# The recurrence of a two-model kernel: second running sum right behind the first, the next step's readers between the two groups of level 1, last-column copies in eight entries

## The chip, the cores and the metric

The kernel runs on one core of a Trainium2 chip. Its engines are TensorE (PE for the matmuls, PEld for the loads of their stationary operand), VectorE (DVE), ScalarE (ACT), GpSimd (POOL) and the queue of SyncE (SP) that issues most transfers. They run side by side and wait for one another by semaphores. The metric is the device time of one execution in microseconds (us), lower is better.

## The reference

The reference is two small models, one after the other. What the change touches is one stage of the first: the RWKV recurrence, run once forward and once backward over 256 context tokens and then 512 image tokens, with a 64x64 state for each of 16 heads.

```python
def wkv_scan(r, decay, k, v, a_vec, b_vec, s0, reverse):
    def step(s, inp):
        r_t, w_t, k_t, v_t, a_t, b_t = inp
        sa = jnp.einsum('bhvk,bhk->bhv', s, a_t)
        s = s * w_t[:, :, None, :] + sa[..., None] * b_t[:, :, None, :] + v_t[..., None] * k_t[:, :, None, :]
        return s, jnp.einsum('bhvk,bhk->bhv', s, r_t)
    ...
            for d in range(N_DIRS):
                reverse = d == 1
                dec_c, k_c, a_c = dirs_c[d]
                yc_d, s_ctx = wkv_scan(r_c, dec_c, k_c, vh_c, -kk_c, kk_c * a_c, s0, reverse)
                dec_x, k_x, a_x = dirs_x[d]
                yx_d, _ = wkv_scan(r_x, dec_x, k_x, vh_x, -kk_x, kk_x * a_x, s_ctx, reverse)
```

## The kernel before

The tokens are cut into chunks of 64: four of context, then eight of the image. A step n (0 to 11) works on a pair of chunks, one of each direction, numbered u = 2n (forward) and u = 2n + 1 (backward). Within a chunk the recurrence is a triangular solve, done by doubling in levels 1 to 5, each level in two groups g of four head pairs. One level of one group is: TensorE's factor (L2427), ScalarE's copies of it out of PSUM (L2251, L2253, L2254), TensorE's update (L2444), VectorE's add of that (L2340) and VectorE's transpose (L2344), which the factor of the next level reads. Below, update(l, g) is that add on VectorE.

While step n goes through its levels, two other things are woven in, by an order that is written out by hand for each engine (`wkv_tensor`, `wkv_scalar`, `wkv_vector`, `wkv_pool`):

- the rest of step n - 1 (`before`): its right sides, its solution, its outputs (L2535 on TensorE; copied by ScalarE at L2273 for the first half of the image, added by VectorE at L2356 for the second) and its new states (L2552; added by VectorE at L2364);
- the preparation of step n + 1 (`after`), for each of its two chunks: `chunk_scan` (a running sum of log decays on VectorE, L2155), `chunk_rise` and `chunk_fall` (the exponentials of it and of its negative on ScalarE, L2108 and L2113), `chunk_readers` on VectorE (a product L2167, in image chunks a second one L2169, and a copy L2171 of the last column into PT), `chunk_writers` (two products, L2182), the score matmuls (L2218), and on GpSimd the masks of the scores (`chunk_mask`, L2094 and L2096, and `chunk_strict`, L2101).

Once a step GpSimd multiplies the states with the last columns (`decay`, L2229). It runs behind the masks in GpSimd's queue and reads PT. PT has four entries, so `chunk_readers` waits for a decay before it writes:

```python
                for step in (last, f"zn{u - 4}"):
                    if later(dve, step):
                        dve.wait_ge(*at(step))
```

`last` is the last output (image) or right side (context) of step n - 1, which reads the same buffer that the readers write. Transfers of a chunk's streams into LD are issued by SP as soon as the writers of that buffer are done; `chunk_scan` waits for them (`ld{u}`).

Of the kernel before, what the change touches and what calls it, by code (L numbers as in the profile page):

```python
# [25 lines left out]
P = 128  # L26
# [10 lines left out]
CH = 64  # L37
# [131 lines left out]
def build(nc, a, out, table):  # L169
# [3 lines left out]
    with ctx:  # L173
# [1831 lines left out]
        def take_scr(*dims):  # L2005
            nonlocal off
            t = S(off, *dims)
            off += int(np.prod(dims))
            return t
# [3 lines left out]
        EM = [EPX[0][:, :, 0:CH], EPX[1][:, :, 1:CH + 1]]  # L2013
        BK = [take_scr(KT, 2, CH) for _ in range(2)]
        MD = take_scr(2, 128)
        PT = take_scr(4, 8)
        assert off <= 12288 + 10 * TA
        off = 12288 + 10 * TA
        ZZ = take_scr(2, 8, CH)
# [137 lines left out]
        def chunk_readers(dve, u, d, c, img, first):  # L2157
            ld = LD[:, d]
            if later(dve, f"rise{u}"):
                dve.wait_ge(*at(f"rise{u}"))  # L2160
            if u >= 4:
                last = f"Y{u - 4}.1" if u - 4 >= 2 * NCHC else f"Q{u - 4}.1"
                for step in (last, f"zn{u - 4}"):
                    if later(dve, step):
                        dve.wait_ge(*at(step))
            r = AR[(u // 2) % 2][d]
            did(V, dve.scalar_tensor_tensor(r[:, :, 0, :], v3(ld[:, 2, :]), -1.0, EM[d], ALU.mult, ALU.mult).then_inc(vector_done, 1))  # L2167
            if img:
                did(V, dve.tensor_tensor(r[:, :, 1, :], v3(ld[:, 5, :]), EP[d], ALU.mult).then_inc(vector_done, 1))  # L2169
            e = CH - 1 if d == 0 else 0  # L2170
            did(V, dve.tensor_copy(PT[:, u % 4, :], EP[d][:, :, e]).then_inc(vector_done, 1))  # L2171

        def chunk_writers(dve, u, d, c, img, first):
            ld = LD[:, d]
# [48 lines left out]
        def wkv_pool(pool):  # L2223
            steps = list(units())

            def decay(u):
                if later(pool, f"free.Z{u}.1"):
                    pool.wait_ge(*at(f"free.Z{u}.1"))
                did(G_, pool.tensor_tensor(ZZ[:, :, :, :], ZZ[:, :, :, :], PT[:, u % 4:u % 4 + 2, :].unsqueeze(3).to_broadcast([P, 2, 8, CH]),  # L2229
                                           ALU.mult).then_inc(pool_done, 1), f"zn{u}")  # L2230
                marks[f"zn{u + 1}"] = marks[f"zn{u}"]
            for n, pair in list(enumerate(steps))[1:]:
                if n >= 2:
                    decay(2 * (n - 2))
                for un in pair:
                    chunk_mask(pool, un, 0)
                    chunk_mask(pool, un, 1)
                for l in range(2, LEVELS):
                    for un in pair:
                        chunk_mask(pool, un, l)  # L2240
                for un in pair:
                    chunk_strict(pool, *un)
            decay(2 * (NCH - 2))

        def wkv_scalar(act):
            def factor(pair, l, g):
                for u, d, c, img, first in pair:
                    t = pairs(tile(act, f"G{u}.{l}.{g}"))
                    out = GT[d][:, 4 * g:4 * g + 4, :]
                    if d == 0:  # L2250
                        did(A_, act.activation(out, t, ACT.Copy).then_inc(scalar_done, 1), f"free.G{u}.{l}.{g}")  # L2251
                    else:
                        did(A_, act.activation(out[rows(0)], t[rows(1)], ACT.Copy).then_inc(scalar_done, 1))  # L2253
                        did(A_, act.activation(out[rows(1)], t[rows(0)], ACT.Copy).then_inc(scalar_done, 1), f"free.G{u}.{l}.{g}")  # L2254

            def right_side(pair, g):
                for u, d, c, img, first in pair:
                    t = tile(act, f"Q{u}.{g}")
                    did(A_, act.activation(QB[d][:, 4 * g:4 * g + 4, :], pairs(t), ACT.Copy).then_inc(scalar_done, 1), f"free.Q{u}.{g}")

            def solution(pair, g):
                for u, d, c, img, first in pair:
                    sv = SV[u // 2 % 2][d]
                    t = pairs(tile(act, f"S{u}.{g}"))
                    for q in range(2):
                        did(A_, act.activation(sv[q][rows(1 - q), 4 * g:4 * g + 4, :], t[rows(1 - q)], ACT.Copy).then_inc(scalar_done, 1))
                    marks[f"free.S{u}.{g}"] = (A_, count[A_])

            def first_outputs(pair, g):
                for u, d, c, img, first in pair:  # L2270
                    if img and first:
                        t = pairs(tile(act, f"Y{u}.{g}"))
                        did(A_, act.activation(YA[:, 4 * g:4 * g + 4, c * CH:c * CH + CH], t, ACT.Copy).then_inc(scalar_done, 1), f"free.Y{u}.{g}")  # L2273

            def keys(u, d, c, img, first):
                for q in range(2):
                    t = tile(act, f"T{u}.{q}")
                    did(A_, act.activation(odd(BKT[d], q), t.rearrange("p (h c) -> p h c", c=CH), ACT.Copy).then_inc(scalar_done, 1), f"free.T{u}.{q}")
            steps = list(units())
            for n in range(NCH + 1):  # L2280
                now = steps[n] if n < NCH else []
                before = steps[n - 1] if n else []
                after = steps[n + 1] if n + 1 < NCH else []
                right_side(before, 0)
                right_side(before, 1)
                solution(before, 0)
                factor(now, 1, 0)
                solution(before, 1)
                first_outputs(before, 0)
                factor(now, 1, 1)  # L2290
                first_outputs(before, 1)
                if after:
                    chunk_rise(act, *after[0])
                    chunk_fall(act, *after[0])
                factor(now, 2, 0)
                if after:
                    chunk_rise(act, *after[1])
                factor(now, 2, 1)
                factor(now, 3, 0)
                if now:  # L2300
                    keys(*now[0])
                factor(now, 3, 1)
                if now:
                    keys(*now[1])
                if after:
                    chunk_fall(act, *after[1])
                factor(now, 4, 0)
                if after:
                    chunk_evict(act, *after[0], (0,))
                factor(now, 4, 1)  # L2310
                if after:
                    chunk_evict(act, *after[0], (1,))
                factor(now, 5, 0)
                if after:
                    chunk_evict(act, *after[1])
                factor(now, 5, 1)

        def wkv_vector(dve):
# [48 lines left out]
            for n in range(NCH + 1):  # L2367
                now = steps[n] if n < NCH else []
                before = steps[n - 1] if n else []
                after = steps[n + 1] if n + 1 < NCH else []  # L2370
                if n and now:
                    chunk_begin(dve, *now[1])
                    first_turn(dve, now)
                update(before, 5, 1)
                if after:
                    chunk_scan(dve, *after[0])
                outputs(before, 0)
                update(now, 1, 0)
                outputs(before, 1)
                update(now, 1, 1)  # L2380
                if after:
                    chunk_scan(dve, *after[1])
                states(before if now else [], 0)
                update(now, 2, 0)
                states(before if now else [], 1)
                update(now, 2, 1)
                if after:
                    chunk_readers(dve, *after[0])
                update(now, 3, 0)
                if after:  # L2390
                    chunk_writers(dve, *after[0])
                update(now, 3, 1)
                if after:
                    chunk_readers(dve, *after[1])
                update(now, 4, 0)
                if after:
                    chunk_writers(dve, *after[1])
                    lower(*after[0], (0,))
                update(now, 4, 1)
                if after:  # L2400
                    lower(*after[0], (1,))
                if after:
                    lower(*after[1], (0,))
                update(now, 5, 0)
                if after:
                    lower(*after[1], (1,))
                    chunk_begin(dve, *after[0])
# [1599 lines left out]
```

## Time and profile before

| | |
|---|---|
| time, 3 runs | median 3513.45 us (3512.17 to 3514.84) |
| the profiled execution | 3511.41 us, span 3509.6 us |
| recurrence in the trace | from about 1205 us to about 1630 us |
| one step | 30.6 us (step 0) to 40.5 us (step 9), by the starts of the first running sum |
| busy over the span | PE 94%, DVE 41%, ACT 33%, POOL 10% |

The share of busy time says little here: PE counts as busy in other stages too, and inside the recurrence four engines take turns. What counts is which result the others are waiting for at a given place of a step. In the trace a step is found by its running sums: step 5, which is shown most below, starts with the one at 1372.34 us.

### The profile page before, as it was taken

To read this page: it belongs to the slowest core of one execution; us is meant where nothing else is said; L and a number is where in the kernel's file an instruction comes from. 1 tells how busy PE (TensorE), PEld (TensorE's weight loads), DVE (VectorE), ACT (ScalarE), POOL (GpSimd) and SP (SyncE) were. 2 spreads that over 40 slices of the span, in tenths; PEclk is the share of its full clock that TensorE was granted. 3 is DMA by queue.
4 is the path that set the end of the run, shared out by engine and by line. 5 is a ranking of instruction groups with operands and counts; after the bars stand their busy time and mean duration, and the time that the engine had idled before them with its cause. 6 is when DMAs were issued, how large, how long until landed. Compare 5 with 4: busy or idle time off the path is not lost.

```text
span 3509.6 us, 63853 instructions
## 1 busy us (share of the span) xinstructions
PE 3294.7 (94%) x28640; PEld 2166.4 (62%) x28640; DVE 1427.5 (41%) x2203; ACT 1163.9 (33%) x2220; POOL 362.9 (10%) x294
## 2 busy tenths in 40 slices
PE   8999999999899998888888888899999999999998
PEld 6665444435458588886342332457788876778886
DVE  3341000024651378785420001467743445764343
ACT  3330111113451477764200001345331324533231
POOL 0010000000200275653000000010000001000000
PEclk9989999999999999999999999999999999999999
DMA  9268999995543444335379999521423212142320
GB/s 373 97 244 332 393 372 385 370 351 197 184 164 117 123 90 98 84 82 184 130 296 419 421 408 421 213 67 55 144 96 93 87 31 68 55 144 96 96 84 24
DMA packets 340209, 674.78 MB, mean 192 GB/s; under 512 B 156616, under 2 KB 248904, under 8 KB 284640
## 3 DMA queue, kind: packets, MB, share of 16 engines
q1 hardware_dynamic: 328048, 633.14, 49.8%
q0 software_dynamic: 5264, 18.68, 1.5%
q10 hardware_dynamic: 6624, 18.88, 1.4%
q8 instruction: 225, 3.69, 0.4%
q14 instruction: 48, 0.39, 0.0%
HBM read 636.04 MB, written 34.60 MB: 191 GB/s over the span
## 4 chain that ended last, share of the span: by engine, by line
PE 78%; DVE 8%; DMA 8%; ACT 3%; POOL 2%; issue 1%; SPq 0%; ACTq 0%; DVEq 0%; POOLq 0%
PE ps L1180 15%; PE ps L1191 5%; DMA ring<-in_moe_wu 4%; PE ps L3578 3%; PE ps L685 3%; PE ps L3577 3%; PE ps L3576 3%; PE ps L686 3%; PE ps L687 3%; PE ps L3595 3%; PE ps L3593 3%; PE ps L3594 3%; PE ps L1727 2%; PE ps L1702 2%; DMA ring<-in_moe_wg 2%; PE ps L769 2%
## 5 line engine op out<-in xcount | busy, mean ns | idle before, releaser
L1180 PE MATMUL ps<-ring,H 128*64 128x512 f32 x2016 | 479.8, 601 | 40.3 <-DMA ring<-in_moe_wu 31.7
L1312 DVE TENSOR_TENSOR scr<-ps,scr 128x512 f32<-128x512 f32 x32 | 22.1, 692 | 884.6 <-PE ps L1180 884.6
L1180 PEld LDWEIGHTS ps<-ring,H 128*64 128x64 f32 x2016 | 150.4, 137 | 324.4 <-issue 237.9
L1180 PE MATMUL ps<-ring,scr 128*64 128x512 f32 x1016 | 244.3, 599 | 29.2 <-DMA ring<-in_moe_wd 25.1
L3558 DVE TENSOR_TENSOR ring_rounded<-ring,scr_rounded 128x2048 fp32r<-128x2048 f32 x64 | 146.7, 2292 | 215.0 <-ACT scr_rounded L3551 214.6
L3578 PE MATMUL ps<-scr_rounded 128*128 128x512 f32 x512 | 203.4, 397 | 0.0
L3593 PE MATMUL ps<-scr_rounded,ring_rounded 128*128 128x512 f32 x512 | 201.6, 394 | 1.7 <-DVE ring_rounded L3558 1.7
L3595 PE MATMUL ps<-scr_rounded 128*128 128x512 f32 x512 | 202.9, 396 | 0.0
L3577 PE MATMUL ps<-H_rounded,scr_rounded 128*128 128x512 f32 x512 | 202.2, 395 | 0.0
L3551 ACT ACTIVATE scr_rounded<-ring 128x2048 fp32r<-128x2048 f32 x64 | 122.1, 1907 | 241.1 <-PE ps L3595 241.1
L3576 PE MATMUL ps<-scr_rounded,ring_rounded 128*128 128x512 f32 x512 | 200.5, 392 | 0.0
L1180 PEld LDWEIGHTS ps<-ring,scr 128*64 128x64 f32 x1016 | 74.5, 137 | 176.3 <-issue 125.9
L1259 ACT ACTIVATE scr<-ps 128x512 f32<-128x512 f32 x32 | 19.1, 597 | 383.2 <-PE ps L1219 383.2
L686 PE MATMUL ps<-H_rounded,ring_rounded 128*128 128x512 f32 (+1 forms) x384 | 143.3, 373 | 0.0
L1269 ACT ACTIVATE scr<-ps 64x512 f32<-64x512 f32 x64 | 37.9, 592 | 287.6 <-PE ps L1180 286.8
L1191 PE MATMUL ps<-ring,H 128*32 128x256 f32 x2048 | 120.3, 381 | 0.0
L687 PE MATMUL ps<-ring_rounded 128*128 128x512 f32 (+1 forms) x320 | 118.5, 370 | 0.0
L3615 ACT ACTIVATE scr<-ps 128x512 f32<-128x512 f32 x64 | 38.3, 598 | 226.8 <-PE ps L3578 226.8
L2427 PE MATMUL ps<-scr,ring 64*64 64x64 f32 x3840 | 93.4, 226 | 20.8 <-issue 9.2
L3577 PEld LDWEIGHTS ps<-H_rounded,scr_rounded 128*128 128x128 f32 x512 | 96.1, 188 | 25.6 <-issue 0.5
L3576 PEld LDWEIGHTS ps<-scr_rounded,ring_rounded 128*128 128x128 f32 x512 | 96.1, 188 | 24.4 <-issue 0.5
L3593 PEld LDWEIGHTS ps<-scr_rounded,ring_rounded 128*128 128x128 f32 x512 | 96.1, 188 | 24.1 <-issue 2.1
(548 smaller groups left out, 6694.6 us busy)
## 6 DMA issues: line engine op xcount, KB each, us to landing
ring<-in_moe_wu SPq DMA_DIRECT2D x128, 1024.0 KB, 9.6
ring<-in_moe_wd SPq DMA_DIRECT2D x127, 1024.0 KB, 10.2
ring<-in_moe_wg SPq DMA_DIRECT2D x124, 1024.0 KB, 9.7
ring<-in_mlp_w SPq DMA_DIRECT2D x64, 1024.0 KB, 5.4
ring<-in_ada_w SPq DMA_DIRECT2D x48, 1024.0 KB, 10.6
ring<-in_w_in SPq DMA_DIRECT2D x14, 1024.0 KB, 5.3
ring<-in_w_out SPq DMA_DIRECT2D x8, 1024.0 KB, 5.3
st_lw<-scr POOLq DMA_DIRECT2D x16, 384.0 KB, 3.9
```

The source lines that it names most:

```text
L685: pe.matmul(out, w[1], x[0], start=start, stop=False)
L686: pe.matmul(rest or out, w[0], x[1], start=False, stop=False)
L687: return pe.matmul(out, w[0], x[0], start=False, stop=stop)
L1180: ins = pe.matmul(bx[64 * n:64 * n + 64, :], stat_x(k), w[:, k % 4, :], start=k == 0, stop=k == KT - 1)
L1191: ins = pe.matmul(bc[32 * n:32 * n + 32, 0:256], stat_c(k), w[:, k % 4, o:o + 256], start=k == 0, stop=k == KT - 1)
L3551: did(A_, act.activation(WHI[j % 2], ring[:, place[name][0], :], ACT.Copy).then_inc(scalar_done, 1), f"wh.{name}")
L3558: did(V, dve.tensor_tensor(ring_r[:, at_slot, :], ring[:, at_slot, :], WHI[j % 2].bitcast(F32), ALU.subtract).then_inc(vector_done, 1), f" ...
L3576: pe.matmul(b, low[:, k, o], hh, start=k == 0, stop=False)
L3577: pe.matmul(b, high[:, k, o], hl, start=False, stop=False)
L3578: ins = pe.matmul(b, high[:, k, o], hh, start=False, stop=k == KT - 1)
L3593: pe.matmul(banks[m], low[:, k, o], hh, start=f == 0, stop=False)
L3595: ins = pe.matmul(banks[m], high[:, k, o], hh, start=False, stop=f == 15)
```

## The change

Four edits, all in the recurrence. On VectorE the running sum of the second chunk (`chunk_scan(dve, *after[1])`) moves from behind update(1, 1) to directly behind that of the first chunk. The readers of the first chunk move from behind update(2, 1) to between update(1, 0) and the outputs and update(1, 1). On ScalarE the rising exponential of the first chunk moves ahead of the second group of the outputs. PT gets eight entries instead of four, and `chunk_readers` waits for the decay eight chunks back, not four.

```diff
-        PT = take_scr(4, 8)
+        PT = take_scr(8, 8)
...
-                for step in (last, f"zn{u - 4}"):
+                for step in (last, f"zn{u - 8}")[0:1 + (u >= 8)]:
...
-            did(V, dve.tensor_copy(PT[:, u % 4, :], EP[d][:, :, e]).then_inc(vector_done, 1))
+            did(V, dve.tensor_copy(PT[:, u % 8, :], EP[d][:, :, e]).then_inc(vector_done, 1))
...
                 factor(now, 1, 1)
+                if after:
+                    chunk_rise(act, *after[0])
                 first_outputs(before, 1)
                 if after:
-                    chunk_rise(act, *after[0])
                     chunk_fall(act, *after[0])
...
                 if after:
                     chunk_scan(dve, *after[0])
+                    chunk_scan(dve, *after[1])
                 outputs(before, 0)
                 update(now, 1, 0)
+                if after:
+                    chunk_readers(dve, *after[0])
                 outputs(before, 1)
                 update(now, 1, 1)
-                if after:
-                    chunk_scan(dve, *after[1])
                 states(before if now else [], 0)
                 update(now, 2, 0)
                 states(before if now else [], 1)
                 update(now, 2, 1)
-                if after:
-                    chunk_readers(dve, *after[0])
                 update(now, 3, 0)
```

VectorE before, from the last update of step 4 to update(3, 0) of step 5 (in the order of the program the running sum is printed as SCALAR_TENSOR_TENSOR at L2155):

```order
L2340 TENSOR_TENSOR scr<-ps,scr 128x512
L2155 SCALAR_TENSOR_TENSOR scr<-scr,H 128x512
L2340 TENSOR_TENSOR scr<-ps,ring 128x512
L2344 STREAM_TRANSPOSE scr<-scr 128x512
L2340 TENSOR_TENSOR scr<-ps,ring 128x512
L2344 STREAM_TRANSPOSE scr<-scr 128x512
L2155 SCALAR_TENSOR_TENSOR scr<-scr,H 128x512
L2364 TENSOR_TENSOR scr<-ps,scr 128x2x256
```

VectorE with the change, the same place (every line behind the edit has one number more, L2341 is the former L2340):

```order
L2341 TENSOR_TENSOR scr<-ps,scr 128x512
L2155 SCALAR_TENSOR_TENSOR scr<-scr,H 128x512 x2
L2341 TENSOR_TENSOR scr<-ps,ring 128x512
L2345 STREAM_TRANSPOSE scr<-scr 128x512
L2167 SCALAR_TENSOR_TENSOR scr<-H,scr 128x8x64
L2169 TENSOR_TENSOR scr<-H,scr 128x8x64
L2171 COPY scr<-scr 128x8
L2341 TENSOR_TENSOR scr<-ps,ring 128x512
L2345 STREAM_TRANSPOSE scr<-scr 128x512
L2365 TENSOR_TENSOR scr<-ps,scr 128x2x256
```

Both running sums now stand ahead of update(1, 0), and the three instructions of the readers stand ahead of update(1, 1).

ScalarE, steps 5 to 8, the one piece that differs (L2254 ends the copies of level 1, L2273 is the outputs' second group):

```order
 L2253 ACTIVATE ring<-ps 64x256
 L2254 ACTIVATE ring<-ps 64x256
+L2108 ACTIVATE scr<-scr 128x8x64
 L2273 ACTIVATE scr<-ps 128x4x64 x2
-L2108 ACTIVATE scr<-scr 128x8x64
 L2113 ACTIVATE scr<-scr 128x512
```

The rising exponential now stands ahead of the two copies of the outputs, so it no longer waits for them. TensorE's and GpSimd's orders are the same.

## Rows read from the trace of the kernel before

**Rows 1.** Waits, 1200 to 1630 us: total us, times, longest us.
```profile
DVE scr L2340 <- PE ps L2444: 61.2, 44, 4.7
...
PEld ps L2427 <- issue: 21.0, 23, 4.4
...
ACT scr L2113 <- DVE scr L2182: 7.0, 9, 1.7
...
DVE X L2167 <- POOL scr L2229: 4.0, 4, 1.6
```

**Rows 2.** Timeline of step 5, all engines: start, length, instruction, [idle before <- releaser].
```profile
1377.65 0.69 DVE L2340 TENSOR_TENSOR scr<-ps,ring 128x512 f32<-128x512 f32 x1 [3.92 <-PE ps L2444]
...
1378.12 0.38 ACT L2254 ACTIVATE ring<-ps 64x256 f32<-64x256 f32 x1
...
1379.28 0.85 ACT L2273 ACTIVATE scr<-ps 128x256 f32<-128x256 f32 x2 [0.79 <-PE ps L2535]
...
1380.83 0.69 DVE L2340 TENSOR_TENSOR scr<-ps,ring 128x512 f32<-128x512 f32 x1 [1.74 <-PE ps L2444]
...
1381.55 0.71 DVE L2344 STREAM_TRANSPOSE scr<-scr 128x512 f32<-128x512 f32 x1
...
1382.19 1.18 DVE L2155 TENSOR_TENSOR_SCAN scr<-scr,H 128x512 f32<-128x512 f32 x1
...
1383.13 0.27 PE L2427 MATMUL ps<-scr,ring 64*64 64x64 f32 x2
...
1386.08 0.69 DVE L2340 TENSOR_TENSOR scr<-ps,scr 128x512 f32<-128x512 f32 x1 [0.21 <-PE ps L2444]
...
1387.96 0.69 DVE L2167 SCALAR_TENSOR_TENSOR X<-H,scr 128x512 f32<-128x512 f32 x1 [0.44 <-POOL scr L2229]
...
1389.17 0.16 DVE L2171 COPY scr<-scr 128x8 f32<-128x8 f32 x1
1389.24 0.68 DVE L2340 TENSOR_TENSOR scr<-ps,scr 128x512 f32<-128x512 f32 x1
...
1391.88 0.63 ACT L2113 ACTIVATE scr<-scr 128x512 f32<-128x512 f32 x1 [0.60 <-DVE scr L2182]
```

**Rows 3.** Timeline of POOL in the same step.
```profile
1366.77 12.95 POOL L2094 TENSOR_TENSOR ring<-scr 128x512 f32<-128x512 f32 x9
1379.67 2.54 POOL L2101 TENSOR_TENSOR scr<-scr 128x512 f32<-128x512 f32 x2
```

**Rows 4.** Timeline of DVE in step 0.
```profile
1208.49 0.69 DVE L2340 TENSOR_TENSOR scr<-ps,ring 128x512 f32<-128x512 f32 x1 [0.34 <-PE ps L2444]
...
1212.47 1.23 DVE L2155 TENSOR_TENSOR_SCAN scr<-scr,H 128x512 f32<-128x512 f32 x1 [1.22 <-DMA H<-st_kk]
...
1216.39 0.69 DVE L2340 TENSOR_TENSOR scr<-ps,scr 128x512 f32<-128x512 f32 x1 [1.36 <-PE ps L2444]
```

**Rows 5.** Timeline of the steps 3 and 9.
```profile
1307.07 0.63 ACT L2108 ACTIVATE scr<-scr 128x512 f32<-128x512 f32 x1
...
1307.82 0.69 DVE L2340 TENSOR_TENSOR scr<-ps,ring 128x512 f32<-128x512 f32 x1 [0.90 <-PE ps L2444]
...
1527.30 0.89 DVE L2356 TENSOR_TENSOR scr<-ps,scr 128x256 f32<-128x256 f32 x2
```

**Rows 6.** Timeline of two later stages, DVE and POOL.
```profile
1648.58 1.27 POOL L2651 TENSOR_TENSOR scr<-scr 128x512 f32<-128x512 f32 x1 [2.93 <-DMA scr<-st_kd]
1648.66 1.74 DVE L2679 SCALAR_TENSOR_TENSOR scr<-scr,cst 128x512 f32<-128x512 f32 x1
...
1653.65 0.75 DVE L2679 SCALAR_TENSOR_TENSOR scr<-scr,cst 128x512 f32<-128x512 f32 x1
...
1749.12 9.27 POOL L1620 TENSOR_TENSOR scr_rounded<-scr,scr_rounded 128x1024 fp32r<-128x1024 f32 x4 [92.70 <-ACT scr_rounded L1462]
...
1756.78 1.89 DVE L1527 TENSOR_SCALAR scr<-scr 16x512 f32<-16x512 f32 x1
```

**Rows 7.** Groups by line and form, DVE: xcount, then busy us, mean ns, idle before.
```profile
L1163 DVE TENSOR_SCALAR scr<-scr,small 16x512 f32<-16x512 f32 x2 | 0.9, 474 | 0.1
```

More of the change, by code:

```diff
@@ L2228, in decay @@
                     pool.wait_ge(*at(f"free.Z{u}.1"))
-                did(G_, pool.tensor_tensor(ZZ[:, :, :, :], ZZ[:, :, :, :], PT[:, u % 4:u % 4 + 2, :].unsqueeze(3).to_broadcast([P, 2, 8, CH]),
+                did(G_, pool.tensor_tensor(ZZ[:, :, :, :], ZZ[:, :, :, :], PT[:, u % 8:u % 8 + 2, :].unsqueeze(3).to_broadcast([P, 2, 8, CH]),
                                            ALU.mult).then_inc(pool_done, 1), f"zn{u}")
```

## The prediction

> **What bounds the kernel now.** I read the waits of the stretch first, then one step's timeline with all engines, then GpSimd alone. The waits [rows 1] show VectorE waiting 61.2 us in 44 places for update matmuls: in most of a step VectorE has time, and only where it is late is a shorter order worth something. Step 5 [rows 2] shows where. VectorE is idle 3.92 us ahead of update(1, 0) and 1.74 us ahead of update(1, 1). Behind update(1, 1) it is busy nearly without a gap: transpose, running sum (1.18 us at 1382.19), states, update(2, 0), and at update(2, 1) a wait of only 0.21 us for TensorE. So the running sum there stood beside TensorE's own chain and cost almost nothing. Then come the readers, 0.44 us late for GpSimd's decay, and update(3, 0) starts at 1389.24 with no wait for TensorE: from here VectorE is what the others wait for. ScalarE stands 0.60 us ahead of L2113 for VectorE's writers. In all steps this last wait is 7.0 us in 9 places [rows 1].
>
> **What the change frees.** It takes the second running sum, the first readers and the wait for the decay out of the late part of a step. What that is worth is not their length but what the next bound leaves. In step 5 update(3, 0) and the writers behind it come earlier, ScalarE can start L2113 as soon as its copies of the keys are done, and that is those 0.60 us; from there the copies of level 4 and TensorE's update of level 4 follow it. So the gain over all steps is 7.0 us, plus what comes earlier because ScalarE no longer waits for the second running sum ahead of its copies of level 2. Working steps 1 and 3 through by their rows in the same way as step 5, I get 0.2 and 0.5 us for that; rounded up for the others, 0.9. Gain: 7.9 us, at least 7.0. The sum in its new place lies in the 3.92 us ahead of update(1, 0) and costs nothing in the steps from 1 on; with that cover gone it would cost its 1.2 us. The eight entries of PT and the copy's new address cost nothing by themselves.
>
> **What it costs in step 0.** There the second running sum starts at 1212.47, when its streams have landed, 1.22 us after VectorE was ready, while both updates of level 1 had been done from 1208.49 on [rows 4]. With the sum ahead of them, update(1, 0) cannot start before 1212.47 + 1.14 = 1213.6, which is 5.1 us later. Everything of levels 1 and 2 is queued behind that instruction. Update(2, 1) had waited 1.36 us behind the same late sum by way of ScalarE; that wait is gone, so 5.1 - 1.4 = 3.7 us remain. Bounds: 3.7 to 5.1.
>
> **What the readers cost in their new place.** Update(1, 1) started at 1380.83 and its transpose ended at 1381.55 + 0.71 = 1382.26; TensorE's factor of the next level came at 1383.13 [rows 2]. So update(1, 1) can be late by 0.87 us before TensorE feels it.
>
> In step 5 the readers must wait for the outputs that read their buffer; ScalarE's row at 1379.28 shows when these are there. The rising exponential, moved ahead, runs from 1378.12 + 0.38 on and is done by then. Alone the three instructions take 1389.24 - 1387.96 = 1.28 us and end at 1380.56, inside the gap. In steps 3 and 4 there is no such cover: the exponential comes at 1307.07 + 0.63 = 1307.70 and update(1, 1) had been at 1307.82 [rows 5], so it slips by 1.2 us. In steps 9 and 10 the outputs of VectorE (L2356, from 1527.30) stand behind the readers, which costs 0.6 us, still under 0.87.
>
> But GpSimd is at work there. Before, the readers ran when its masks were done; now they run at 1379.3 to 1382, and the masks and strict masks fill 1366.77 to 1382.2 [rows 3], some 1.2 us more once the second sum runs beside them. Two rows show what an op with two inputs in SBUF does beside a GpSimd product [rows 6]: the same L2679 takes 0.75 us alone and 1.74 us when GpSimd's 1.27 us product began at 1648.58, 0.08 us ahead of it. It stood still for 0.99 us. So I charge 0.5 us for the first product of a chunk's readers (it meets a GpSimd op half way on the mean) and 1.0 us for a second one, since GpSimd's next mask is queued and starts when the first product ends.
>
> For the copy of the last column the rows don't decide. It took 0.16 us [rows 2], always with GpSimd idle or behind it. Of ops with one input, the transpose kept its 0.71 us while GpSimd ran [rows 2, 3], but L1527 took 1.89 us beside GpSimd's products [rows 6], where a tensor-scalar op of the same 16x512 took 0.474 [rows 7]. A copy from SBUF to SBUF is nearer to L1527 than to the transpose, so I charge it one wait of 1.0 us; bounds 0 and 1.4.
>
> The Trainium skill has a rule for this place, and it speaks against the change: "SBUF — State Buffer", section "SBUF: two separate sides", says that VectorE and GpSimd share a port pair under an exclusive lock, which a VectorE op takes when it has two SBUF inputs or is in a two-port mode, and that the loser stands still for a whole instruction. "VectorE: DVE Perf Modes", section "What auto-detection actually checks", puts a one-source op with source and destination in SBUF into such a mode, a copy too. By these the copy is held as well; L2679 and L1527 agree. By the idle rows alone the readers would cost no more than their 1.28 us, and the sum would be the faster rival below.
>
> Lateness of update(1, 1), less the 0.87 us, and less what steps 3 and 4 pay even unheld (0.35 us, already in the gain):
> - steps 1 and 2 (one product and a copy): 0.6 + 0.5 + 1.0 = 2.1, so 1.25 each, 2.5
> - steps 3 and 4: 1.2 + 1.5 + 1.0 = 3.7, so 2.5 each, 5.0
> - steps 5 to 8: 1379.28 + 1.28 + 2.5 = 1383.06, which is 2.23 late, so 1.36 each, 5.4
> - step 9: 0.6 + 2.5 = 3.1, so 2.2; step 10, where GpSimd's work ends before the copy, 1.2: 3.4
> Together 16.3 us, of which 9.0 are the copies. Bounds: 0 (nothing held) and about 26 (each product held for a whole 1.0 us, 12 in all, and ten copies for 1.4 us, 14).
>
> **The sum.** 3.7 + 16.3 - 7.9 = 12.1 us slower, on the profiled execution's 3511.41 us: 3523.5, say 3524. The median of the runs lies 2.0 us above that execution, which is inside the range. A later end of the recurrence moves all stages behind it by the same, since they start from its result. Bounds of the sum: 3.7 - 7.9 = -4.2, and 5.1 + 26 - 7.0 = +24.
>
> **The rivals.**
> Products held, copy free: 3.7 + 7.3 - 7.9 = 3.1 us slower, 3514.5 (3516.6 against the median). For it speaks that the copy has only 8 elements and steps through its source; against it L1527.
> Faster: nothing is held, because the readers' first product finds GpSimd's queue drained or goes ahead of it. Then the sum is 4.2 us faster, 3507. It turns at the place of the readers: when update(1, 1) slips by no more than 0.87 us in each step, the gain stands. Against it speaks that GpSimd's rows fill just that window.
> Swallowed by TensorE's own stalls: its factor waits 21.0 us in 23 places for nothing that the profile shows [rows 1]. Where update(1, 1) comes late such a stall can fall into the wait, and the loss shrinks; where the late part gets shorter, a stall can take the gain. I take this as 3 us either way, so a total near +9 or near 0 by which part it meets.
>
> **How the numbers follow.** A measurement of this kernel tells 0.2%, 7.0 us, from no change. Forecast (products and copy held, 9 to 18 us slower): 0.50. Products held alone, 0 to 7 slower: 0.27. Nothing held, 1 to 6 faster: 0.10. Stalls: 0.13, half of it within 0.2%, the rest parted. So faster by over 0.2%: 0.08 (only nothing held with some luck of the stalls); within: 0.36 (products held with the copy free, part of the case with nothing held, half of the stalls); slower: 0.56. The likeliest case alone is 3520 to 3530. The range of 8 in 10 reaches down over the second rival and up for longer holds: 3513 to 3531.
>
> **What the profile after would show.** Right: update(1, 0) of step 0 five microseconds later, behind a wait of the running sum for its transfer; L2167 and L2169 of the first chunk at 1.2 to 1.8 us in place of 0.65 to 0.69, L2171 at about 1.2 us once per step; VectorE without a wait at update(1, 1) in steps 5 to 8, and TensorE's factor of level 2 waiting for VectorE's transpose; the wait of L2167 for L2229 gone; ScalarE's wait ahead of L2113 gone. Wrong: if L2167 keeps its 0.65 us, nothing is held and the faster rival stands; if only L2171 keeps its 0.16 us, the products alone are held. A loss with short readers would mean that a wait that I don't see (streams not landed for the second sum in later steps) has taken their place.

## The result, and the profile after

The changed kernel takes 3530.3 us (median of 12 runs, 3518.5 to 3538.3), the kernel before 3512.1 us beside it: ratio 1.0050, 95% interval 1.0041 to 1.0059, so 17.6 us slower (14.4 to 20.7). Timed a second time, among the experiments below, it was 13.7 us slower (ratio 1.0039, 1.0025 to 1.0053; 8.8 to 18.6). The profiled execution took 3530.9 us, span 3529.1 us.

The waits of the recurrence after the change (1200 to 1650 us, since it now ends later), in the columns of [rows 1]:

```profile
DVE scr L2341 <- PE ps L2444: 49.3, 47, 3.7
PEld ps L2427 <- issue: 24.2, 21, 4.4
...
PE ps L2427 <- DVE scr L2345: 20.2, 10, 5.0
...
DVE scr L2155 <- DMA H<-st_kk: 4.7, 2, 4.2
...
DVE scr L2155 <- DMA H<-st_r: 1.8, 3, 0.8
```

L2341, the update, waits 49.3 us for TensorE where it (as L2340) waited 61.2. In exchange there is a wait that the kernel before hardly had (0.3 us in one place): TensorE's factor, L2427, stands 20.2 us in 10 places for VectorE's transpose L2345. The waits of L2113 for the writers and of L2167 for the decay L2229 are gone. VectorE's timeline shows where TensorE's new wait comes from, first in step 0 (to be read against [rows 4]), then in step 5 (against [rows 2]):

```profile
1205.34 1.23 DVE L2155 TENSOR_TENSOR_SCAN scr<-scr,H 128x512 f32<-128x512 f32 x1 [0.44 <-DMA H<-st_kk]
1210.80 1.23 DVE L2155 TENSOR_TENSOR_SCAN scr<-scr,H 128x512 f32<-128x512 f32 x1 [4.24 <-DMA H<-st_kk]
1211.94 0.67 DVE L2341 TENSOR_TENSOR scr<-ps,ring 128x512 f32<-128x512 f32 x1
...
1384.79 4.27 DVE L2155 TENSOR_TENSOR_SCAN scr<-scr,H 128x512 f32<-128x512 f32 x2
1390.58 0.69 DVE L2341 TENSOR_TENSOR scr<-ps,ring 128x512 f32<-128x512 f32 x1 [1.52 <-PE ps L2444]
1391.31 0.71 DVE L2345 STREAM_TRANSPOSE scr<-scr 128x512 f32<-128x512 f32 x1
1392.20 0.95 DVE L2167 SCALAR_TENSOR_TENSOR X<-H,scr 128x512 f32<-128x512 f32 x1 [0.18 <-PE ps L2535]
1393.08 1.76 DVE L2169 TENSOR_TENSOR X<-H,scr 128x512 f32<-128x512 f32 x1
1394.76 1.24 DVE L2171 COPY scr<-scr 128x8 f32<-128x8 f32 x1
1395.91 0.68 DVE L2341 TENSOR_TENSOR scr<-ps,ring 128x512 f32<-128x512 f32 x1
...
1400.29 0.69 DVE L2341 TENSOR_TENSOR scr<-ps,scr 128x512 f32<-128x512 f32 x1 [0.39 <-PE ps L2444]
1401.02 0.71 DVE L2345 STREAM_TRANSPOSE scr<-scr 128x512 f32<-128x512 f32 x1
1402.73 0.69 DVE L2341 TENSOR_TENSOR scr<-ps,scr 128x512 f32<-128x512 f32 x1 [1.00 <-PE ps L2444]
```

In step 0 VectorE stands 4.24 us for the second sum's transfer, and only then comes update(1, 0). In step 5 the product L2169 takes 1.76 us and the copy L2171 1.24 us, which took 0.68 and 0.16 us before; update(1, 1) starts without a wait. Further on update(3, 0) waits 1.00 us for TensorE where before it had no wait: the late part did get shorter. GpSimd in the same step:

```profile
1381.65 12.64 POOL L2094 TENSOR_TENSOR ring<-scr 128x512 f32<-128x512 f32 x8
1394.24 2.95 POOL L2101 TENSOR_TENSOR scr<-scr 128x512 f32<-128x512 f32 x2
```

Its masks fill the time up to 1397.2, the readers' time with it. The two strict masks (L2101) take 2.95 us where they took 2.54 before [rows 3], so GpSimd is held in its turn.

**A measure by place.** To part the terms I take from VectorE's timeline the time from the start of update(1, 0) to that of update(3, 0); in step 5 it was 1389.24 - 1377.65 = 11.59 us before and is 1402.73 - 1390.58 = 12.15 us now. Both ends are the same instructions in every kernel, and the readers lie inside, in their old place or their new one. Added over steps 1 to 10 it is 114.3 us before and 125.2 us after the change; the second profile of the changed kernel gives 125.7. In the table below, kernels that differ in nothing or in step 0 alone agree within 1.5 us, which shows how far one execution can be trusted here. From update(3, 0) to the next step's first sum, added over steps 0 to 9, it is 191.3 us before and 190.8 after: no gain or loss shows there, though this part scatters more (186.8 to 193.4 us over all kernels below). Of a step this leaves the stretch from its first sum to update(1, 0): in steps 1 to 10 it is 50.7 us before, 58.0 after and 53.1 in the second profile of the change. In e5, which leaves both sums in their old places, it is 52.8, and in the other ten kernels below, all with the sum moved, 51.2 to 55.0. So up to 7 us of the difference between two executions lie there, and these profiles don't tell whether the sum's place has a part in it.

### The profile page after: what moved, and what is told of

It reads as the page before. It is cut to its first block, busy times and chain, and to the rows that moved or that the text cites. A ratio compares the mean times of both kernels' runs of the same rounds, so it can differ in the third digit from the quotient of the medians.

```text
span 3529.1 us, 63849 instructions
## 1 busy us (share of the span) xinstructions
PE 3298.6 (93%) x28640; PEld 2165.6 (61%) x28640; DVE 1458.2 (41%) x2203; ACT 1164.7 (33%) x2220; POOL 376.4 (11%) x294
## 4 chain that ended last, share of the span: by engine, by line
PE 79%; DVE 8%; DMA 8%; ACT 2%; issue 1%; SPq 1%; ACTq 0%; POOL 0%; DVEq 0%; POOLq 0%
PE ps L1180 15%; PE ps L1191 5%; DMA ring<-in_moe_wu 4%; PE ps L3578 3%; PE ps L685 3%; PE ps L3577 3%; PE ps L3576 3%; PE ps L686 3%; PE ps L687 3%; PE ps L3595 3%; PE ps L3593 3%; PE ps L3594 3%; PE ps L1727 2%; PE ps L1702 2%; DMA ring<-in_moe_wg 2%; PE ps L2444 2%
## 5 line engine op out<-in xcount | busy, mean ns | idle before, releaser
L1259 ACT ACTIVATE scr<-ps 128x512 f32<-128x512 f32 x32 | 19.1, 597 | 381.8 <-PE ps L1219 381.8
L2427 PE MATMUL ps<-scr,ring 64*64 64x64 f32 x3840 | 94.0, 228 | 42.8 <-DVE scr L2345 20.2
```

## The experiments

All times in the table are against the kernel before, run on the same chip, by the ratio and its interval; the last column is the measure just described, from one profiled execution each.

| run | edit | us against before | update(1, 0) to (3, 0), steps 1 to 10 |
|---|---|---|---|
| before | | 0 | 114.3 |
| after | | +17.6 (+14.4 to +20.7) | 125.2 |
| e9_same | the same again | +13.7 (+8.8 to +18.6) | 125.7 |
| e1_scan | before, second sum moved | +2.1 (-2.1 to +6.0) | 111.4 |
| e5_eight | before, eight entries | -3.5 (-7.4 to 0) | 112.9 |
| e2_readers_back | after, readers back | -1.1 (-5.6 to +3.9) | 109.7 |
| e7_back_step0 | after, readers and step 0 back | -3.2 (-8.1 to +1.4) | 110.5 |
| e4_step0 | after, step 0 back | +13.3 (+9.1 to +17.2) | 126.7 |
| e3_copy_late | after, first copy back | +4.2 (0 to +8.4) | 112.2 |
| e6_reduce | after, copy as a reduction | +2.5 (-1.4 to +6.3) | 113.6 |
| e10_reduce_step0 | e6 and step 0 back | -1.1 (-5.3 to +3.5) | 112.4 |
| e8_short_masks | after, GpSimd's masks short | -3.5 (-7.4 to +0.7) | 106.8 |
| e12_masks_wait | after, masks wait for readers | -2.1 (-6.0 to +1.8) | 107.6 |
| e11_masks_wait_step0 | e12 and step 0 back | -2.5 (-6.3 to +1.1) | 108.6 |

**Which part costs: e1_scan, e2_readers_back.** The first moves only the sum, the second puts only the readers back:

```diff
 e1_scan, from before
+                    chunk_scan(dve, *after[1])     behind chunk_scan(dve, *after[0])
-                    chunk_scan(dve, *after[1])     behind update(now, 1, 1)
 e2_readers_back, from after
-                    chunk_readers(dve, *after[0])  behind update(now, 1, 0)
+                    chunk_readers(dve, *after[0])  behind update(now, 2, 1)
```

> The kernel before with the second running sum alone moved behind the first; readers, copies and the four entries stay. Held-readers theory: only step 0 pays, where the sum's wait for its transfer now stands ahead of update(1, 0) and TensorE waited 4.7 us more for VectorE; 3515 to 3518 us, 3 to 6 above before. Rival (the sum in its new place is itself what costs, because it is held by GpSimd or waits for its loads in every step): 3525 us or more. Rival (TensorE's own issue stalls fall differently in each kernel): anything within 3 us of before.

> The changed kernel with the first readers put back behind update(2, 1); both sums, the earlier exponential and the eight entries stay. Held-readers theory: the 12.9 us of the steps from 1 on go, step 0's 4.7 stay, less what the late part of a step gains now that the decay isn't waited for; 3509 to 3517 us. Rival (the sum's place is what costs): 3525 us or more.

The sum alone costs 2.1 us, 6.0 at most by the interval. That is less than the 3 to 6 us that I had expected, and inside the 3 us of the rival of TensorE's stalls; in e1's trace step 0 does pay 4.0 us from its first sum to update(3, 0), and the measure by place is 2.9 us below before. With the readers back nothing of the 17.6 us is left (3511.9 us, as expected), though step 0 pays its price there too: the measure by place is 4.6 us below before. The rival that the sum's place is what costs falls. The readers carry the loss.

**Step 0: e4_step0.**

```diff
-                    chunk_scan(dve, *after[1])
+                    if n:
+                        chunk_scan(dve, *after[1])
...
                 update(now, 1, 1)
+                if after and not n:
+                    chunk_scan(dve, *after[1])
```

> The changed kernel, but in step 0 the second running sum keeps its old place behind update(1, 1). Theory (the sum's wait for its transfer holds update(1, 0) in step 0): 4 to 6 us less than the changed kernel, 3524 to 3526 us. Rival (step 0's delay is given back later, or it is stalls of TensorE's issue that made step 0 longer): within 2 us of the changed kernel.

3524.6 us, 4.2 us less than the change as first timed; against the second timing it is 0.4 us, so the time alone doesn't show it. In its timeline the second sum of step 0 waits 0.29 us for its transfer, and update(1, 0) stands ahead of it:

```profile
1208.48 0.69 DVE L2341 TENSOR_TENSOR scr<-ps,ring 128x512 f32<-128x512 f32 x1
...
1212.77 1.23 DVE L2155 TENSOR_TENSOR_SCAN scr<-scr,H 128x512 f32<-128x512 f32 x1 [0.29 <-DMA H<-st_kk]
```

The traces show it plainly. From the first sum to update(3, 0) step 0 takes 11.4 to 12.9 us in the six kernels with the sum behind (before, e4, e5, e7, e10, e11) and 15.9 to 17.2 us in the eight profiles with it ahead.

**The copy: e3_copy_late, e6_reduce.** The first takes the copy out of the readers and puts it, for the first chunk, behind update(2, 1). The second leaves it in place and takes another instruction for it:

```diff
 e3_copy_late, from after: chunk_last holds the copy that chunk_readers loses
                 update(now, 2, 1)
+                if after:
+                    chunk_last(dve, *after[0])
...
                     chunk_readers(dve, *after[1])
+                    chunk_last(dve, *after[1])
 e6_reduce, from after
-            did(V, dve.tensor_copy(PT[:, u % 8, :], EP[d][:, :, e]).then_inc(vector_done, 1))
+            did(V, dve.tensor_reduce(PT[:, u % 8, :], EP[d][:, :, e:e + 1], AX, ALU.add).then_inc(vector_done, 1))
```

> The changed kernel with the copy of the last column alone moved back behind update(2, 1); the two products stay in their new place. If the ten copies held for 1.08 us each lie on the path, 7 to 10 us less than the changed kernel: 3520 to 3523 us. If the copy's standstill is swallowed (GpSimd's lock then only falls on the next operation), no more than 2 us less: 3528 us or more.

> The changed kernel with the copy of the last column made by a tensor_reduce over one element, in the same place; everything else as changed. By the two-port theory (the copy is held because it runs in a mode that takes the port shared with GpSimd) the reduction isn't held: its row is under 0.3 us, and the time falls by 9 to 13 us to 3516 to 3521 us. Rival (any operation behind the held product stands still in that place, whatever its form): its row stays at 1.2 us and the time at 3527 us or more.

Both take most of the loss away, 13.4 and 15.1 us against the first timing of the change and 9.5 and 11.2 us against the second; e3 more than I had expected by the first. All instances of L2171 in the changed kernel (ns: least, median, most):

```profile
L2171 DVE COPY scr<-scr x22: 158/166/1244, 1213.8 to 1601.4; 128x8 f32<-128x8 f32 x22
```

and in e6_reduce:

```profile
L2171 DVE TENSOR_REDUCE scr<-scr x22: 151/155/160, 1212.1 to 1584.4; 128x8 f32<-128x8 f32 x22
```

The same eight elements, in the same place beside the same GpSimd masks, take 160 ns at most as a reduction and up to 1244 ns as a copy. The second product ahead of it is held in e6 as well (1.76 to 1.77 us in all eight steps). In the one step from 1 on in which the copy went free, step 6, GpSimd's last mask had ended at 1434.1 and the copy started at 1434.57. So it is not the place and not being queued behind a held product, but what the copy asks for. The Trainium skill, "SBUF — State Buffer", section "Who interferes with whom", says that a copy can enter a two-port mode and contend with GpSimd, while a tensor_reduce cannot on trn2; the trace agrees with both halves.

**GpSimd itself: e8_short_masks, e12_masks_wait.** e8 makes GpSimd's masks of levels 1 to 5 and its strict masks over one head pair of eight, so it leaves out seven eighths of that work. e12 leaves nothing out, but holds GpSimd's masks of level 5 and its strict masks back until the first chunk's readers are done:

```diff
 e8_short_masks, from after
-                ins = pool.tensor_tensor(NM[d][l], score, mask.unsqueeze(1).to_broadcast([P, 8, CH]), ALU.mult)
+                ins = pool.tensor_tensor(NM[d][l][:, 0:1, :], score[:, 0:1, :], mask.unsqueeze(1).to_broadcast([P, 1, CH]), ALU.mult)
...
+            did(G_, pool.tensor_tensor(ka[:, 0:1, :], ka[:, 0:1, :], MD[:, d, 0:CH].unsqueeze(1).to_broadcast([P, 1, CH]), ALU.mult)
 e12_masks_wait, from after
-            did(V, dve.tensor_copy(PT[:, u % 8, :], EP[d][:, :, e]).then_inc(vector_done, 1))
+            did(V, dve.tensor_copy(PT[:, u % 8, :], EP[d][:, :, e]).then_inc(vector_done, 1), f"read{u}")
...
                 for l in range(2, LEVELS):
+                    if l == LEVELS - 1 and n + 1 < NCH and later(pool, f"read{pair[1][0] + 1}"):
+                        pool.wait_ge(*at(f"read{pair[1][0] + 1}"))
```

> The changed kernel with GpSimd's masks of levels 1 to 5 and its strict masks made over one of eight head pairs, so seven eighths of that masking are left out (the times of the other engines' work do not depend on it); instructions and waits are the same. If GpSimd's operations hold both products and the copy, L2167, L2169 and L2171 fall to 0.65, 0.68 and 0.16 us in the steps from 1 on and the time by 13 to 18 us, to 3512 to 3517 us. If the products are late by themselves and only the copy is held: 3518 to 3522 us. If nothing is held by GpSimd: 3528 us or more.

> As the run before it in this list, but with the second sum of step 0 where the change puts it: 4 us more than that run, 3507 to 3512 us, some 20 us less than the changed kernel. Rival as there.

Both give back all of it, e8 1.3 us more than the most I had expected. Products in the changed kernel, both chunks' instances of the X buffer:

```profile
L2167 DVE SCALAR_TENSOR_TENSOR X<-H,scr x10: 648/684/1777, 1247.3 to 1559.3; 128x512 f32<-128x512 f32 x10
L2169 DVE TENSOR_TENSOR X<-H,scr x8: 681/1219/1764, 1315.6 to 1559.9; 128x512 f32<-128x512 f32 x8
```

in e8_short_masks, with the running sums and the copies:

```profile
L2155 DVE TENSOR_TENSOR_SCAN scr<-scr,H x22: 1194/1215/1372, 1206.9 to 1560.1; 128x512 f32<-128x512 f32 x22
...
L2167 DVE SCALAR_TENSOR_TENSOR X<-H,scr x10: 648/670/693, 1247.1 to 1541.4; 128x512 f32<-128x512 f32 x10
...
L2169 DVE TENSOR_TENSOR X<-H,scr x8: 680/682/685, 1311.6 to 1542.0; 128x512 f32<-128x512 f32 x8
...
L2171 DVE COPY scr<-scr x22: 158/164/166, 1214.4 to 1580.6; 128x8 f32<-128x8 f32 x22
```

and in e12_masks_wait:

```profile
L2169 DVE TENSOR_TENSOR X<-H,scr x8: 679/682/686, 1311.7 to 1539.7; 128x512 f32<-128x512 f32 x8
...
L2171 DVE COPY scr<-scr x22: 155/165/1246, 1213.8 to 1579.1; 128x8 f32<-128x8 f32 x22
```

where the waits have a new line of GpSimd's:

```profile
POOL ring L2094 <- DVE scr L2171: 19.1, 8, 4.1
```

In e8 nothing of the readers is held any more. In e12 the second product is free in all steps, the first product and the copy from step 5 on; in steps 1 to 4, where masks of lower levels still run beside the readers, the first product takes up to 1.59 us (step 4) and the copy 1.24 and 1.25 us in steps 1 and 2. GpSimd stands 19.1 us in 8 places, and no other engine's waits for it grew by more than 0.2 us against the changed kernel. The readers stayed where the change put them, so the overlap with GpSimd is the cause and not the place.

**The sum of it: e7_back_step0, e9_same, e10_reduce_step0, e11_masks_wait_step0, e5_eight.** e7 joins the edits of e2 and e4, e10 those of e6 and e4, e11 those of e12 and e4; e9 has none. e5 has the change's edits of PT alone, on before:

```diff
-        PT = take_scr(4, 8)
+        PT = take_scr(8, 8)
...
-                for step in (last, f"zn{u - 4}"):
+                for step in (last, f"zn{u - 8}")[0:1 + (u >= 8)]:
```

> The changed kernel with the readers back behind update(2, 1) and, in step 0 alone, the second sum back in its old place; eight entries, earlier exponential and the earlier sum from step 1 on stay. If step 0's price (4.2 us when measured with the readers in their new place) and the readers' price add up: 3.5 to 6.5 us below before, 3504 to 3507 us. Rival (step 0's delay is given back when the readers stand late): as with the readers back alone, within 1.5 us of before.

> The kernel before with the eight entries of PT alone, so that the first readers no longer wait for GpSimd's decay; all instructions keep their places. If the wait for the decay is what made ScalarE wait ahead of L2113, and that wait is worth time: 3 to 7 us below before, 3504 to 3508 us. Rival (TensorE's own chain of level 3 hides it): within 2 us of before.

> The changed kernel itself, timed beside the three below on one chip, to part the copies' price from the scatter between chips: 14 to 21 us above before, as it was.

> The changed kernel with the last column taken by the tensor_reduce that isn't held, and the second sum of step 0 in its old place. If the two prices add up (15 us for the copies, 4.2 for step 0): 19 us less than the changed kernel, 3509 to 3513 us, within 3 us of before. If by the trace's own waits the copies are worth no more than 9.6 us: 3514 to 3519 us.

> The changed kernel with GpSimd made to wait for the first chunk's readers ahead of its masks of level 5 and its strict masks, and the second sum of step 0 in its old place; nothing is left out. If it is the overlap with GpSimd and not the place that holds the readers, L2167, L2169 and L2171 keep 0.65, 0.68 and 0.16 us and the gain comes through: 3503 to 3508 us, the fastest kernel of this study. If the later masks are needed sooner (strict masks and the decay then come 4 us later): 3510 us or more, with waits for GpSimd on VectorE or TensorE.

e10 lies 14.8 us below the change timed beside it, between my two expectations. e7 and e11 came out at 3511.0 and 3510.6 us and e5 at 3512.5, some us above what I had expected of them. By their medians they lie where their rivals had them, but the longer waits for GpSimd that e11's rival calls for are not in its trace, and for e7 and e5 the times don't decide. Their ratios lie 2.5 to 3.5 us below before with intervals that reach to no difference (e5's just ends there). So no version here beats the kernel before by what a measurement can tell. In the traces of e4, e7, e10 and e11 step 0 is 4 to 6 us shorter than in those of the kernels that differ from them in this alone, but how much of that reaches the time is left open: e11 and e12 differ by 0.4 us where I had expected 4.

## Why the prediction was nearly right, and what it left out

The sign and the mechanism held, and 3530.3 us is inside the range, at its upper end; the second timing lies 1.6 us above the sum. By its own steps:

- **Step 0, +3.7.** Right by the traces: from the first sum to update(3, 0) step 0 grew from 1.56 + 11.36 to 6.60 + 10.35 us, 4.0 more. By the times e4 gives 4.2 or 0.4, by which timing of the change is taken.
- **The sum in its new place, 0 from step 1 on.** Not contradicted by e1, whose 2.1 us hold step 0 too, but not shown either, since the stretch ahead of update(1, 0) scatters by up to 7 us. The pair of sums takes 3.5 to 4.5 us there, held by GpSimd as well (the median in e8 is 1.215 us for one), and waits up to 0.8 us for a load in three steps. In step 5 it is covered, as I had said, by the wait ahead of update(1, 0), 1.52 us of which is left.
- **Readers held.** By rows: the first product takes 0.7 to 1.8 us, 0.50 us longer than 0.67 on the mean of ten steps (charged: 0.5); the second one 1.75 to 1.76 us in all eight steps that have it, 1.08 longer (charged: 1.0); the copy 1.22 to 1.24 us in nine steps of ten, 1.06 to 1.08 longer (charged: 1.0 in all but step 10; it was step 6 that went free, and step 10 in the second profile). In step 5 update(1, 1) comes 2.15 us later behind update(1, 0) than before (charged: 2.23), and TensorE stands 1.13 us for it (charged: 1.36). Each was sized rightly.
- **Readers' loss, 16.3 in all.** By the measure by place it is 125.5 (mean of the two profiles) less 108.1 (mean of e11 and e12), 17.4 us; less e8's 106.8, where nothing is held, it is 18.7. The copies are 125.5 less 113.0 (mean of e6 and e10), 12.5 where I had 9.0, and the products the other 4.9 (by e8: 6.2) where I had 7.3.
- **The gain, 7.9.** By the same measure 114.3 less 108.1, 6.2 us (by e8: 7.5). ScalarE's wait ahead of L2113 is gone as forecast, and I counted it in full; behind update(3, 0), where it stood, no gain shows (191.3 and 190.8 us).
- **The sum, +12.1.** With these sizes it is 17.4 + 4.0 - 6.2 = 15.2 us (the same by e8), between the two timings of 13.7 and 17.6. It leaves out the stretch ahead of update(1, 0), which was 7.3 and 2.4 us longer in the two profiles of the change. That the forecast of 12.1 came this near is in part luck: the copies were priced too low and the products too high, and the two errors go against each other.

The rival of the copy going free falls with L2171's rows, the faster one with all of them. Its condition was made true in e8: with nothing held that kernel lies 3.5 us below before, where 4.2 was worked out, but its interval of -7.4 to +0.7 does not part it from no change.

**The step that failed** is the price of the copies, and what it lacked, as far as the measure by place shows, is TensorE's clock. Between update(1, 0) and update(1, 1) the copies cost 9.0 us (53.8 on the mean of the two changed profiles, 44.8 of e6 and e10), as charged. The other 3.5 us lie behind update(1, 1), where in e6 update(3, 0) follows after 6.82 us in each step. In the changed kernel it is 6.82 us in most steps too, but 8.34, 8.08 and 8.34 in steps 3, 4 and 10. TensorE in step 3, and in step 5 below it:

```profile
1319.86 0.69 PE L2427 MATMUL ps<-scr,ring 64*64 64x64 f32 x32 [3.33 <-DVE scr L2345]
1320.49 1.00 PE L2552 MATMUL ps<-H,ring 128*64 128x64 f32 x16
1321.27 1.07 PE L2552 MATMUL ps<-scr,ring 128*64 128x64 f32 x16
1322.27 1.87 PE L2444 MATMUL ps<-scr,ring 64*64 64x64 f32 x30
...
1397.39 0.69 PE L2427 MATMUL ps<-scr,ring 64*64 64x64 f32 x32 [1.13 <-DVE scr L2345]
1398.02 0.69 PE L2552 MATMUL ps<-H,ring 128*64 128x64 f32 x16
1398.53 0.64 PE L2552 MATMUL ps<-scr,ring 128*64 128x64 f32 x16
1399.10 1.09 PE L2444 MATMUL ps<-scr,ring 64*64 64x64 f32 x30
```

and the windows of the same stretch and of step 4 (the first number behind POOL's busy time is the granted clock):

```profile
1316.00:1319.80 3.80, 0.53 (x19) 0.39 (x14) 3.77 (x5) 0.27 (x1) 3.80 (x4) 1.00 0.02 4
1319.80:1322.20 2.40, 2.34 (x64) 2.23 (x64) 1.89 (x4) 1.14 (x3) 1.11 (x1) 0.68 0.00 0
1322.20:1324.60 2.40, 2.40 (x68) 2.28 (x64) 1.01 (x2) 0.00 (x0) 1.44 (x1) 0.61 0.26 59
1324.60:1327.00 2.40, 2.36 (x86) 2.13 (x80) 1.36 (x3) 2.18 (x5) 0.46 (x1) 1.00 0.71 163
...
1358.50:1361.00 2.50, 2.28 (x54) 2.16 (x56) 2.06 (x4) 1.06 (x3) 0.02 (x1) 0.50 0.03 7
```

TensorE waited 3.33 us for the late transpose, and the matmuls behind the wait ran slower: L2444's thirty take 1.87 us there, and 1.09 us in step 5 (last rows), behind a wait of 1.13 us. The granted clock had fallen from 1.00 to the lower of its two levels (0.50 in the window of step 4, 1.2 GHz). Where that happens the wait is paid for twice, once as itself and once as about 1.5 us of slow matmuls. In e6, where TensorE waits 1.3 us in step 3, the clock stays whole:

```profile
1312.50:1315.00 2.50, 2.38 (x86) 2.24 (x88) 2.46 (x5) 1.14 (x3) 2.50 (x3) 1.00 0.00 0
```

Not every such wait is followed by a fall. In the changed kernel the clock stays whole behind 1.98 us in step 9, though it falls behind 1.82 us in step 10; in its second profile it falls in steps 4 and 5, behind 3.34 and 1.81 us, but not in step 3 (a row of its timeline and the window behind it):

```profile
1322.75 0.69 PE L2427 MATMUL ps<-scr,ring 64*64 64x64 f32 x32 [2.52 <-DVE scr L2345]
...
1322.70:1326.00 3.30, 3.25 (x128) 3.05 (x129) 2.88 (x5) 1.14 (x3) 1.75 (x2) 1.00 0.01 3
```

The clock also falls in the kernel before, where no transpose is that late, for instance behind a stretch in which TensorE was busy for 0.47 of 2.40 us:

```profile
1268.00:1270.40 2.40, 0.47 (x16) 0.33 (x13) 2.30 (x4) 0.38 (x1) 2.40 (x3) 1.00 0.02 3
1270.50:1273.80 3.30, 3.30 (x90) 3.30 (x90) 0.90 (x1) 2.99 (x8) 3.30 (x3) 0.50 0.03 5
```

From step 1 to update(3, 0) of step 10 it does so 3 times before, 7 and 3 times in the two profiles of the change, and twice in e6 and in e10. So the 3.5 us are where the rows put them, but that the change makes the clock fall more often over the whole recurrence is not shown, and no run changed the clock by itself. Nor does it explain why the two timings of the change differ: their profiled executions took 3530.9 and 3530.6 us. I had put scatter of a few us down to TensorE's issue stalls alone. Added over steps 0 to 11, those of TensorE are 29.8 us before and 30.6 after.

## What to carry to other kernels

Before VectorE work is moved into a gap, look at what GpSimd does in that gap: beside GpSimd's masks an operation with two inputs in SBUF, or a plain copy within SBUF, was held for up to 1.1 us, however short it was itself, and one queued behind a held one was held again in nearly every step. Where it must stay, a form that isn't held (here a reduction over one element) or a pause of GpSimd where nobody waits for it took the loss away here, though no such version came out faster than the kernel before. And where TensorE waits longer for such a delay, its granted clock is to be looked at behind the wait, not only the wait.

## What was not expected of the hardware

- The size of a held instruction did not matter here, which the rows of before had left open: a copy of 128x8 elements, 0.16 us alone, stood 1.08 us, as long as a product of 128x512.
- Two running sums beside GpSimd's masks took 4.27 us (step 5), and VectorE still stood 1.52 us for TensorE behind them.
- Behind a wait of 3.33 us of TensorE its granted clock fell to half, and thirty matmuls of 64x64 took 1.87 us in place of 1.09; behind one of 2.52 us it stayed whole.
